# Norm ahead of the second block's products, and ScalarE instead of VectorE emptying its projection and gate banks

## The reference, cut to what matters

```
xn = rmsnorm(x, norm1_g[l])              # x * rsqrt(mean(x*x) + 1e-6) * g
h  = xn @ w_in[l]                        # 5920 columns, split over four mixers
y_a, y_b, y_c, y_d = gdn(h), diff(h), swa(h), mlstm(h)
branch = einsum('bsnw,nwd->bsnd', ys, w_branch[l])
gate   = sigmoid(einsum('bsd,dne->bsne', xn, w_gate[l]))   # 4 x 1024 columns
x = x + sum(gate * branch, axis=2) @ w_out[l]
xn = rmsnorm(x, norm2_g[l])
x = x + square(relu(xn @ w_mlp1[l])) @ w_mlp2[l]
```

## Time and profile before

| | us |
|---|---|
| median of 3 runs (lowest, highest) | 4129.35 (4128.23, 4131.54) |
| the profiled execution's own time | 4124.45 |
| span of its trace | 4122.7 |
| mean granted clock of PE, share of full | 0.919 |
| PE, DVE and ACT busy, share of the span | 86%, 55%, 33% |
| first `layer_two` pass, from the stream's first instruction | 1089.0 to 2588 |
| stretch alone; Gdn; Diff; Swa; Mlstm; the rest | 114; 457; 206; 138; 148; 436 |

### The profile page before, as it was taken

How to read it: one execution, slowest core, us unless ns; L and a number is a source line. 1 busy time by engine, 2 the same in 40 slices (tenths; PEclk the granted TensorE clock), 3 DMA queues, 4 the chain that set the end, 5 groups by cost and what they waited for, 6 DMA issues and landing times. The chain is left out here.

```text
span 4122.7 us, 48497 instructions
## 1 busy us (share of the span) xinstructions
PE 3533.6 (86%) x17648; PEld 2905.9 (70%) x17648; DVE 2286.6 (55%) x4342; ACT 1380.9 (33%) x2570; POOL 579.9 (14%) x450
## 2 busy tenths in 40 slices
PE   7887888878689999778879999889998779789997
PEld 5666667666567888556757888668887557567886
DVE  3566634656437875567754333348875657663333
ACT  3313333133323333333434332233332334434321
POOL 1000010000103333111111110103333100112110
PEclk9988889888899999899989999999999889889999
DMA  4620036311253222222223333442222212323332
GB/s 127 179 85 28 19 97 171 90 37 31 57 146 105 77 66 62 67 59 78 81 74 105 96 96 92 108 138 72 84 69 80 59 51 61 106 83 91 97 97 72
DMA packets 554066, 350.06 MB, mean 85 GB/s; under 512 B 73412, under 2 KB 497348, under 8 KB 553564
## 3 DMA queue, kind: packets, MB, share of 16 engines
q1 hardware_dynamic: 553820, 346.84, 29.7%
HBM read 301.36 MB, written 45.42 MB: 84 GB/s over the span
## 5 line engine op out<-in xcount | busy, mean ns | idle before, releaser
L556 PE MATMUL bank<-h,w_hi 128*128 128x512 f32 x2240 | 963.0, 430 | 193.6 <-DVE w_low L549 158.6
L557 PE MATMUL bank<-h,w_hi 128*128 128x512 f32 x2240 | 910.2, 406 | 0.0
L558 PE MATMUL bank<-h,w_low 128*128 128x512 f32 x2240 | 908.5, 406 | 0.0
L543 ACT CAST w_hi<-w 128x1024 fp32r<-128x1024 f32 (+2 forms) x456 | 432.5, 950 | 826.2 <-DMA w<-in_w_mlp 395.3
L556 PEld LDWEIGHTS bank<-h,w_hi 128*128 128x128 f32 x2240 | 441.8, 197 | 313.9 <-DVE w_low L549 169.8
L549 DVE TENSOR_TENSOR w_low<-w,w_hi 128x1024 fp32r<-128x1024 f32 (+2 forms) x456 | 528.9, 1161 | 85.2 <-ACT w_hi L543 80.1
L558 PEld LDWEIGHTS bank<-h,w_low 128*128 128x128 f32 x2240 | 439.9, 196 | 102.7
L557 PEld LDWEIGHTS bank<-h,w_hi 128*128 128x128 f32 x2240 | 442.8, 198 | 92.4 <-issue 9.5
L557 PE MATMUL bank<-yT_low,w_hi 128*128 128x512 f32 x768 | 314.3, 409 | 0.0
L1161 ACT ACTIVATE prob<-bank,softmax_stat 128x512 f32<-128x512 f32 (+3 forms) x256 | 145.0, 567 | 293.0 <-DVE softmax_stat L1193 227.2
L556 PE MATMUL bank<-yT_low,w_hi 128*128 128x512 f32 x384 | 166.3, 433 | 56.6 <-DVE xT L685 43.1
(11 more groups left out here) (420 smaller groups left out, 6142.9 us busy)
## 6 DMA issues: line engine op xcount, KB each, us to landing
w<-in_w_in SPq DMA_DIRECT2D x148, 512.0 KB, 4.2
w<-in_w_mlp SPq DMA_DIRECT2D x128, 512.0 KB, 4.0
z<-z_tile SPq DMA_DIRECT2D x164, 256.0 KB, 4.1
w<-in_w_gate SPq DMA_DIRECT2D x64, 512.0 KB, 4.1
q_twice<-z SPq DMA_DIRECT2D x128, 128.0 KB, 2.9
w<-in_w_branch SPq DMA_DIRECT2D x64, 256.0 KB, 2.9
k_twice<-z SPq DMA_DIRECT2D x88, 128.0 KB, 3.7
w<-in_w_out SPq DMA_DIRECT2D x32, 256.0 KB, 2.8
```

Source lines behind the costliest of these rows:

```text
L543: self.a.copy(self.wh[s][:, 0:d, 0:n], self.w[s][:, 0:d, 0:n]).then_inc(self.w_high.sem, 1)
L556: self.t.matmul(bank[0:n, :], wh, high, start=j == 0, stop=False)
L557: self.t.matmul(bank[0:n, :], wh, low, start=False, stop=False)
L558: return self.t.matmul(bank[0:n, :], wl, high, start=False, stop=j == self.depth(i) - 1)
```

## The change

The norm is made first: ACT squares the eight tiles and PE adds them up in one bank by eight matmuls against ones (L853); `root_act` follows at once. DVE then writes `x·g·rstd` into eight tiles of `yT` (L1013), ACT rounds each to `hH` (L937) and DVE subtracts for `hL` (L1019), and the products start on normed activations. So a `z` or gate bank needs no multiplication: `copy_out` (L889) takes it out on ACT, a plain copy for `z` (L895), the Tanh straight out of the bank for a gate (L897). It is written at the head of unit i for unit i-1, ahead of `split_high(i + 1)`. DVE's drain skips these units, POOL's adds go, and everyone who waited for `drained` or `opened` of such a unit (PE, SP's store, the branch drain) waits for `copied`. Behind the change line numbers after L1000 or so are 12 higher.

```diff
...
+    def done(self, i):
+
+        return (self.copied if self.units[i][0] in ("z", "gate") else self.drained).nth(self.order[i])
...
     def pe(self):
+        for j in range(KD):
+            self.t.wait_ge(*self.squared(j))
+            m = self.t.matmul(self.bank[0][:, :], self.k.tab("ones"), self.k.yT[:, j, :], start=j == 0, stop=j == KD - 1)
+        m.then_inc(self.summed.sem, 1)
         for i, (kind, s, e) in enumerate(self.units):
             depth = self.depth(i)
             self.t.wait_ge(*self.w_low(i))
             if i >= 2:
-                self.t.wait_ge(*self.drained(i - 2))
+                self.t.wait_ge(*self.done(i - 2))
...
+    def copy_out(self, i):
+
+        if i >= 0 and self.units[i][0] in ("z", "gate"):
+            n, r = self.width(i), self.row[self.units[i]]
+            row, bank = self.rows[r % 3][0:n, :], self.banks[i % 2][0:n, :]
+            self.a.wait_ge(*self.multiplied(i))
+            self.wait_row_free(self.a, r)
+            if self.units[i][0] == "z":
+                self.a.copy(row, bank).then_inc(self.copied.sem, 1)
+            else:
+                self.a.activation(row, bank, ACT.Tanh, scale=0.5).then_inc(self.copied.sem, 1)
...
     def act(self):
-        self.gained_act(range(2))
+        self.squares_act(range(KD))
+        self.root_act(self.bank[0])
         self.split_high(0)
-        self.gained_act(range(2, KD))
-        self.squares_act(range(KD))
+        for j in range(KD):
+            self.a.wait_ge(*self.normed(j))
+            self.a.copy(self.k.hH[:, j, :], self.k.yT[:, 8 + j, :]).then_inc(self.high.sem, 1)
         for i, (kind, s, e) in enumerate(self.units):
             if e == 0 and (kind == "gate" and s < 3 or kind == "branch" and s == 3):
                 self.branch_high(s)
+            self.copy_out(i - 1)
             if self.pieces(i) == 4:
                 yield
                 self.split_high(i + 1)
-                if i == 1:
-                    self.root_act(self.bank[0])
...
-        if kind in ("z", "gate"):
-            if i == 0:
-                self.v.wait_ge(*self.rooted(0))
-            self.wait_row_free(self.v, r)
-            self.v.tensor_tensor(row[0:n, :], bank[0:n, :], self.k.rstd[0:n, :], ALU.mult).then_inc(self.drained.sem, 1)
-            return
...
     def dve(self):
-        self.gained_dve(range(2))
-        self.split_low(0)
-        self.gained_dve(range(2, KD))
+        self.v.memset(self.eps[:, :], EPS).then_inc(self.eps_set.sem, 1)
+        self.v.wait_ge(*self.g_in(0))
+        self.v.wait_ge(*self.rooted(0))
+        for j in range(KD + 1):
+            if j < KD:
+                self.v.scalar_tensor_tensor(self.k.yT[:, 8 + j, :], self.k.xT[:, j, :], self.g[:, j:j + 1], self.k.rstd[:, :],
+                                            ALU.mult, ALU.mult).then_inc(self.normed.sem, 1)
+            if j == 1:
+                self.split_low(0)
+            if j:
+                self.v.wait_ge(*self.high(j - 1))
+                self.v.tensor_tensor(self.k.hL[:, j - 1, :], self.k.yT[:, 7 + j, :], self.k.hH[:, j - 1, :].bitcast(F32),
+                                     ALU.subtract).then_inc(self.low.sem, 1)
...
     def pool(self):
-        self.gained_pool()
...
```

More of the change, by code:

```diff
@@ L748, in __init__ @@
         self.init_woven(k.A["norm1_g_2"][l])
-        self.opened = self.sig("gate_opened", 4 * KD)
+        by_act = [kind in ("z", "gate") for kind, _, _ in self.units]
+        self.order = [by_act[:i].count(by_act[i]) for i in range(len(self.units))]
+        self.copied = self.sig("copied", sum(by_act))
+        self.normed = self.sig("x_normed", KD)
         self.gate_in = [self.sig(f"gate_in{i}", 3, by=16) for i in range(3)]
@@ L808, in wait_row_free @@
         elif s == 0:
-            eng.wait_ge(*self.drained(self.at[kind, s, e]))
+            eng.wait_ge(*self.done(self.at[kind, s, e]))
         else:
@@ L825, in store @@
             n = self.width(i)
[L826 to L829, removed]
+            self.s.wait_ge(*self.done(i))
             out = (self.k.z2 if kind == "z" else self.k.z3)[e * P:e * P + n, :]
@@ L898, in x_high @@
         if kind == "out":
-            self.a.wait_ge(*self.drained(i))
+            self.a.wait_ge(*self.done(i))
             self.second.gained_act([e])
@@ L965, in drain @@
     def drain(self, i):
-        if i < 0:
+        if i < 0 or self.units[i][0] in ("z", "gate"):
             return
         kind, s, e = self.units[i]
-        n, bank = self.width(i), self.banks[i % 2]
+        bank = self.banks[i % 2]
         self.v.wait_ge(*self.multiplied(i))
@@ L981, in drain @@
             return
-        r = self.row[kind, s, e]
-        row = self.rows[r % 3]
-        if kind in ("z", "gate"):
-            if i == 0:
-                self.v.wait_ge(*self.rooted(0))
-            self.wait_row_free(self.v, r)
-            self.v.tensor_tensor(row[0:n, :], bank[0:n, :], self.k.rstd[0:n, :], ALU.mult).then_inc(self.drained.sem, 1)
-            return
+        row = self.rows[self.row[kind, s, e] % 3]
         acc = self.mixed[:, e, :]
@@ L993, in drain @@
         else:
-            self.v.wait_ge(*self.opened.nth(KD + s * KD + e))
+            self.v.wait_ge(*self.done(self.at["gate", s, e]))
         if s == 0:
```

10 lines of the change are left out of this document (3 added, 7 removed).

## The result

The changed kernel takes 4108.24 us (median of 6 runs, 4104.98 to 4115.22) beside 4128.79 for the kernel before (6 runs, 4121.60 to 4137.47): ratio 0.995, interval 0.9936 to 0.9965.

The account below looks back on a forecast made before the run. PE, busy 86%, was taken to set the pace. From the profiled 4124.45 us, opening +1.3 and mixers −6.0 gave 4119.7; that execution lay 4.9 under the median, so the forecast was 4124.6, range 4112 to 4141.

Parts of the forecast that it names:

- Opening: Start of each pass: norm ahead of the products makes unit 2 end later, +0.2 and +1.1 us, together +1.3.
- The stop of 3.61: Opening: PE's stop ahead of unit 2, where both drains wait for `rstd`, was to go.
- The 18 drains in the stretch alone: Units running before the mixers, 5.44 us of PE each: moving their drains to ACT gains 0, covered by slack.
- The 61 drains: Drains beside the mixers: 14 stand ahead of PE gaps; claimed −3.0 us a pass, ends −8.4 and +4.8.
- I call the nine even: 0: Mixers: nine of those 14 drains lie on paths through ACT; relief and copy cancel, ends −5.4 and +4.8.
- rival 1: Mixers: all of DVE's relief reaches PE, all 14 drains count, 4113.9 us; chance 0.22.
- The term for `M`: Mixers: five drains ahead of the three gaps on `M` give 5 × 0.60 = 3.0 of 3.4 us a pass.
- the example of the second head: Gdn, PE's 1.01 gap: rounding and exponentials behind ACT's copy make DVE's mask some 0.5 us later.
- 14 × 0.60 = 8.4: Mixers: at most 0.60 us freed by each of 14 drains ahead of PE gaps, at most −8.4 a pass.
- Rival 2: Mixers: the wait for a unit's end moves from DVE to ACT, delaying rounding and exponentials; 4153 us, chance 0.12.
- Rival 3: Opening: PE stays at the 1.2 GHz level through unit 1 in both passes; 4134.8 us, chance 0.11.
- Rival 4: Mixers: nothing to gain there, only the opening counts; 4130.7 us, chance 0.18.

Follow-up runs that it names:

- round_first: The changed kernel with ACT's copy out of a bank moved behind the rounding of the next weights: 4094.08 us, 0.9929.
- the four kernels of each kind: Four profiled kernels with a 128x512 DVE row at each of the 79 drain places, four without: mixers 986.4 and 978.5 us a pass.
- both_moves: The changed kernel with a shorter opening (one summing matmul, early weights, high-half passes first) and the copy behind the rounding: 4099.33 us, 0.9929.
- m_gap: The changed kernel with one more DVE product ahead of the first `M` in Gdn's first head; one profiled execution, that head 96.07 us in the first pass.
- the second set of runs: Later repeat of the changed kernel beside the kernel before, both unedited: changed kernel 4112.41 us, ratio 0.9972.
- opening_fast: The changed kernel with DVE adding the squares, one summing matmul, unit 0's weights split early and its high-half passes first: 4110.79 us, 0.9961.
- dve_work: The changed kernel with a DVE product of two SBUF tiles at each of the 79 old drain places, without the drain's wait: 4133.01 us, 1.0027.

## Why the prediction was wrong

**Opening: right in kind, too small.** Forecast +0.2 and +1.1 at unit 2's end, measured +1.1 and +1.8. The term that was mis-sized is the 12.2 us from memset to first scaled row, taken from the stage `Norm`: 13.2 here, since PE's sums took 9.88 us at a granted 0.72 and not 8.83 at 0.81. The 12.2 was itself one execution's value: in the other 13 traces these sums of the stage `Norm` took 7.13 us at 1.00, so that the error came out small by luck. The single matmul that the old opening had was hidden, the eight sums are not. The stop of 3.61 went as forecast. In stage length the opening costs 2.1 and 2.8, since the last low half ahead of Gdn's memset now also stands behind a copy and a rounding; round_first, which has the same norm but the rounding ahead of the copy, is at 114.4 and 114.2.

**The 18 drains in the stretch alone: right** as to the pitch. The copies of units 1 and 2 stand 5.44 apart, as before.

**The 61 drains: the step that failed is "I call the nine even: 0".** The mixers gained 7.9 a pass, not 3.0. The total that came nearest is that of rival 1 (8.4), and it came near by another way. Two things were wrong in the step.

First, the relief at the nine was larger than what ACT took back. Averaged over the four kernels of each kind, PE's waits on DVE fell by 6.9 a pass: on low weight halves by 0.8 in Gdn, 0.8 in Diff and Swa and 1.0 in Mlstm, on `M` by 1.0 and not by 3.0, on other rows of DVE by some 3. Waits on a DMA rose by 1.6 and those on ACT by 0.8, so that PE's idle time fell by 4.5. The term for `M` was too large: the gap of 1.81 lost 0.61, one drain's worth, the next, of 1.37, only 0.07. The price on ACT is real: the example of the second head came out as worked, and round_first, which takes the copy off the rounding's way, gains another 6.5 (978.5 to 972.0, mean of round_first and both_moves). So without that price the drains are worth some 14 a pass, and my 14 × 0.60 = 8.4 was no bound: in those two kernels PE's waits on DVE alone are 10.7 under the 136.6 of the four kernels with a DVE row. It counted only drains in a run of DVE that was unbroken ahead of a gap; that this is why it was too small is likely, but was not tried.

Second, the sum priced a gap at its idle time and put PE's clock in the mixers at nothing. Of the 7.9, 4.5 is idle time and 3.4 is PE's busy time for the same products (Gdn −2.4, Diff and Swa +0.9, Mlstm −1.9). Half of it is the first head of Gdn, busy 88.8 us on average with a DVE row and 87.1 without, at the clocks given under m_gap. m_gap shows it the other way round there, in one trace, though not in both passes right behind the gap; for Mlstm no run shows what the busy time hangs on.

**The sum.** The opening as +2.2 (114.0 to 116.2, means of the two traces of each kernel) and the mixers as −7.9, each taken twice, make −11.4 in two passes. That is inside the interval of the second set of runs (−6 to −17 us) and short of the first (−14 to −26). The −20.5 of the first set is more than the stage lengths explain; what the rest is stays open, though the first block alone varies by as much, see below, and the mixers vary too: taken by pairs of traces, the first set gives −24.3 in the mixers of both passes and +4.9 in the openings, the later set −4.6 and +3.7. Gdn alone, at −4.3 a pass, stayed under the 5 us that the prediction had set as the sign of rival 1.

**The rivals.** Rival 1's size, as said, by another way: not 14 drains at 0.60 each, but more relief, a price on ACT, and PE's busy time. Rival 2's mechanism is there (44.1 us of waits at ACT's copies, the second head's gap +0.5), but it costs some 6.5 a pass and the drains' relief is twice that; ACT's wait did not reach PE whole. ACT is busy 178 of 451 us in Gdn; that its spare time is the reason was not tried. Rival 3: not in the change (unit 1 at 1.00), but in opening_fast. Rival 4 falls: a DVE that was 70% busy in its fullest stage gave 4.3 us in that stage. The Trainium skill ("Perfetto Trace Analysis", section "Optimizing Scalar/DVE Operations") says that offloading may make sense if DVE is saturated; that it gives nothing otherwise was the prediction's own reading and not the page's. Here the rows that stood in DVE's queue ahead of a gap counted, not the mean share.

## What to carry to other kernels

Before taking work off an engine at 55 or 70%, list the gaps of the bounding engine that end on it, and price each removed row there; if the bounding engine is PE, its busy time can fall too, as it did here by 3.4 of 7.9 us. Where the work goes matters as much: an instruction that waits for the end of a product, written ahead of a rounding that needn't wait, cost nearly as much as the change gained (6.5 against 7.9 us a pass), and one moved line gave it back. Moved further, it made PE wait for the bank: look at the waits of the bounding engine on the new place as well. Compare such edits by stage lengths of several traces, and times over many runs.

## What the runs showed of the hardware that was not expected

The first block, which no kernel here edits, ended between 1068 and 1089 us in the profiled executions. PE's granted clock differs there; 150 to 300 us in the kernel before, which reached the second block at 1070.0:

```profile
150.00:300.00 150.00, 123.76 (x592) 100.08 (x591) 92.03 (x177) 32.52 (x59) 0.88 (x2) 0.89 0.37 96
```

and in opening_fast, which reached it at 1089.3:

```profile
150.00:300.00 150.00, 126.80 (x578) 105.38 (x577) 88.28 (x171) 29.61 (x54) 0.88 (x2) 0.84 0.37 96
```

PE is busier, at 0.84 instead of 0.89, and the trace has fewer matmuls in the same 150 us. This window was at 0.84 in the five traces that reached the second block at 1080.9 or later, and at 0.88 or 0.89 in the nine that reached it at 1077.5 or earlier. Differences of 10 us between two kernels' times can come from there, whatever was edited; why one execution is granted less was not tried.

The product of two SBUF tiles on DVE took 1.77 us beside POOL's rows (m_gap), and 0.68 as the median of the same instruction in dve_work. There 28 of the 158 rows ran beside a row of POOL, with a median of 0.95 and up to 1.80; the 130 others took at most 0.69. The Trainium skill ("Perfetto Trace Analysis", section "Optimizing Scalar/DVE Operations") says that GpSimd and DVE share an SBUF read port; the rows agree, and no run here separates the port from other causes. A drain, which reads a bank, had taken 671 to 693 ns wherever it stood, beside POOL too.
